# Suffix sums of stick-breaking attention: products of a rounded high and a low part in place of plain fp32 products

## The chip, the cores and the metric

The kernel runs on one NeuronCore of a Trainium2 chip. The metric is the device time of one execution in microseconds (us). TensorE (PE in the profile, with its weight loads as PEld), VectorE (DVE), ScalarE (ACT), GpSimd (POOL) and SyncE (SP, which issues the weight loads from memory) work from queues of their own, in order, and wait for each other on semaphores.

## The reference, cut to what matters

Two transformer blocks on 256 tokens of width 1024, in fp32. The change is in one mixer of the second block, stick-breaking attention with 8 heads of 128:

```
z = einsum('bqhd,bkhd->bhqk', q[:, lo:hi], k[:, :hi]) * scale
strict = arange(hi)[None, :] < (lo + arange(BLOCK_Q))[:, None]
log_fail = where(strict, -softplus(z), 0.0)
excl = cumsum(log_fail, axis=3, reverse=True) - log_fail
a = where(strict, exp(log_sigmoid(z) + excl), 0.0)
out = einsum('bhqk,bkhd->bqhd', a, v[:, :hi])
```

The reversed cumulative sum over the keys is the suffix sum. The kernel takes it as a product with a fixed 128x128 matrix: keys lie on the partitions, queries along the free axis, and each entry of the product is minus the sum of the softplus values of the keys from its own on.

## The kernel before, in words

The work is a list of phases; each phase has a method for each engine, and each engine goes through the phases in order. Weight products are made from two fp32r parts of each operand (`mm3`, lines 429 to 431: high by high, high by low, low by high). ScalarE rounds a chunk of weights of 128x2048 (L371), VectorE subtracts to get the low part (L379), and TensorE uses the chunk; four chunks are in the ring.

The phase of the change is `Stick`. Per head g it has causal tiles of 384 columns: 256 queries against the first 128 keys, 128 queries against the last 128 keys. The stages of a head are:

- `score`, TensorE (L2071, L2072): the logits, into bankA.
- `mask`, VectorE (L2163): adds the mask, into `lg`.
- ScalarE (L2138 to L2140): Abs, Exp, Ln, into `pt`; then `soften`, VectorE (L2174): the softplus value, in `pt`.
- `suffix`, TensorE (L2081 to L2083): three fp32 products with the suffix matrix and the matrix of minus ones.
- `exponent`, VectorE (L2169): `lg` plus the sums; then ScalarE (L2151): Exp, the attention weights.
- `value`, TensorE (L2097, L2098); after a pair of heads `take_hi` (ScalarE, L2103) and `take_lo` (VectorE, L2109) split the output.

The queues are written out by hand, a loop over g on each engine. In step g TensorE does score g+1, a filler, suffix g, value g-1. VectorE does exponent g-1, soften g, mask g+1, then the low part of a weight chunk (in steps 0, 1, 3, 5, 8) or `take_lo`; in step 7 soften stands ahead of the exponent. ScalarE does Abs, Exp, Ln of head g, in step 0 the rounding of a chunk, then the weights of head g-1 (which wait for exponent g-1), then the copies (L1604) and chunk roundings of the fillers, then `take_hi`; in step 7 a filler's copy stands ahead of the weights.

The fillers are the value and key projections of the next memory attention (`Fill`): one quarter, 12 products of 512 columns, in TensorE's queue before the loop and in each of the steps 0 to 6. Step 7 has none, and no score, since score 7 is in step 6. Step 8 has the transposes of the keys (L1598), ahead of value 7. After the phase comes `sb_out`, the output projection, with products of 512 columns again.

Of the kernel before, what the change touches and what calls it, by code (L numbers as in the profile page):

```python
# [17 lines left out]
F32 = mybir.dt.float32  # L18
F32R = mybir.dt.float32r
I32 = mybir.dt.int32  # L20
ALU = mybir.AluOpType
ACT = mybir.ActivationFunctionType
AX = mybir.AxisListType

P = 128
S = 256
# [12 lines left out]
H2, HD2 = 8, 128  # L39
# [73 lines left out]
C_ID, C_CAUSAL, C_STRICT, C_SUFFIX, C_ONES, C_FREQ, C_BUCK = 0, 128, 384, 768, 896, 1024, 1056  # L113
# [119 lines left out]
def build(nc, dram, out):  # L233
    ctx = ExitStack()
    with ctx:
        def sb(name, shape, dt=F32):
            return ctx.enter_context(nc.sbuf_tensor(name, shape, dt))

        def sem(name):
            return ctx.enter_context(nc.semaphore(name))  # L240
# [15 lines left out]
        qt = sb("qt", [P, KC, S])  # L256
        kt = sb("kt", [P, KC, S])
        v = sb("v", [P, NT, D])
        pet = sb("pet", [P, 6, S])
        rel = sb("rel", [P, 16, S])  # L260
        mem = rel[:, 8:16].rearrange("p (t a) s -> p t (a s)", t=NT)
# [3 lines left out]
        pt = sb("pt", [P, 2, TW])  # L265
        score = sb("score", [P, NT, S])
        const = sb("const", [P, C_BUCK])
# [10 lines left out]
        wi = sb("wi", [P, NT, NPARTS])  # L278
        trig = sb("trig", [P, 2, NT, HALF])
        pos = sb("pos", [P, 4])  # L280

        ps = ctx.enter_context(nc.psum_tensor("ps", [P, 8, TW], F32))
        bankA = [ps[:, 0], ps[:, 1]]
        bankT = [ps[:, 2], ps[:, 3]]
# [37 lines left out]
        def own(eng, counter, ins):  # L322

            eng.wait_ge(counter.sem, counter.inc(ins))
# [87 lines left out]
        def next_hi(act, n):  # L412

            if n + RING < len(PLAN):
                split_hi(act, n + RING)

        def next_lo(dve, n):
            if n + RING < len(PLAN):
                split_lo(dve, n + RING)
# [47 lines left out]
        def norm_scalar(act, name, half):  # L467
            for pair in (2 * half, 2 * half + 1):
                pair_scalar(act, name, pair)
# [10 lines left out]
        def rms_scalar(act, name):  # L480

            c = 2 * NORM[name]
            source_ready(act, name, 1)
            for t in range(NT):
                last = nc.scalar.activation(lg[:, :, :].rearrange("p a n -> p (a n)"), h[:, t], ACT.Square,
                                            scale=D ** -0.5, accum_out=ms[:, c + t:c + t + 1])
                if t == 0:
                    own(act, act_own, last)
            last.then_inc(ms_ready, 1)
# [86 lines left out]
        class Ffn:  # L576
# [274 lines left out]
            def scalar(self, act):  # L851
                if not self.gated:
                    next_hi(act, self.n0)
                rms_scalar(act, self.name)
                if self.gated:
                    next_hi(act, self.n0)
                if self.gated and self.name != "ffn1":
                    nc.scalar.preload_act_table(ACT.Silu)
                if self.gated:
                    act.wait_ge(rs_ready, RMS_AT[self.name])  # L860
                else:
                    act.wait_ge(ms_ready, RMS_AT[self.name])
                self.take_up_scalar(act, 0)
                for c in range(1, 4):
                    next_hi(act, self.n0 + c)
                if self.name == "ffn1":
                    tables.bias_scalar(act)
                for i in range(1, self.steps):
                    self.step_scalar(act, i, self.n0 + 4 * i)
                    if self.name == "ffn1" and i == 3:  # L870
                        tables.scalar(act)
                    if self.name == "ffn2" and i == 3:
                        mem_root.squares(act)
                if not self.following:
                    return
                chunks = [self.n0 + 4 * self.steps + c for c in range(4)]
                for half, n in enumerate(chunks[:2]):
                    next_hi(act, n)
                    norm_scalar(act, self.following, half)
                if self.following == "mla":  # L880
                    next_hi(act, chunks.pop(2))
                if self.following:
                    rms_scalar(act, self.following)
                for n in chunks[2:]:
                    next_hi(act, n)
# [751 lines left out]
        def fill_steps(fillers, g):  # L1637

            return [(f, step) for f in fillers for step, at in enumerate(f.groups) if at == g]
# [412 lines left out]
        class Stick:  # L2052
            def __init__(self, name, need, fillers):

                self.need, self.fillers = need, fillers
                self.scores = sem(name + "_scores")
                self.masked = sem(name + "_masked")
                self.logs = sem(name + "_logs")
                self.soft = sem(name + "_soft")
                self.sums = sem(name + "_sums")  # L2060
                self.expo = sem(name + "_expo")
                self.weights = sem(name + "_weights")
                self.summed = sem(name + "_summed")
                self.hi = sem(name + "_hi")
                self.lo = sem(name + "_lo")
# [7 lines left out]
                                 start=True, stop=True).then_inc(self.scores, 1)  # L2073

            def suffix(self, pe, g):
                pe.wait_ge(self.soft, g + 1)
                if g >= 2:
                    pe.wait_ge(self.expo, g - 1)
                suffix, ones = const[:, C_SUFFIX:C_SUFFIX + P], const[:, C_ONES:C_ONES + P]
                bank = bankT[g % 2]  # L2080
                nc.tensor.matmul(bank[:, 0:S], suffix, pt[:, g % 2, 0:S], start=True, stop=False)  # L2081
                nc.tensor.matmul(bank[:, P:S], ones, pt[:, g % 2, S:S + P], start=False, stop=True)
                nc.tensor.matmul(bank[:, S:S + P], suffix, pt[:, g % 2, S:S + P],  # L2083
                                 start=True, stop=True).then_inc(self.sums, 1)

            def pair_bank(self, pair):
                return bankD[0][pair % 2]
# [41 lines left out]
                        self.value(pe, g - 1)  # L2129

            def scalar(self, act):
                for g in range(H2 + 2):
                    if g < H2:
                        e = pt[:, g % 2, 0:S + P]
                        act.wait_ge(self.masked, g + 1)
                        if g >= 2:
                            act.wait_ge(self.sums, g - 1)
                        own(act, act_own, nc.scalar.activation(e, lg[:, g % 2, 0:S + P], ACT.Abs))  # L2138
                        own(act, act_own, nc.scalar.activation(e, e, ACT.Exp, scale=-1.0))
                        nc.scalar.activation(e, e, ACT.Ln, bias=one[:]).then_inc(self.logs, 1)  # L2140
                    if g == 0:
                        next_hi(act, self.last_chunk)
                    for filler, step in fill_steps(self.fillers, g):
                        if step == 8:
                            filler.scalar(act, step)
                    if 1 <= g <= H2:
                        b = (g - 1) % 2
                        act.wait_ge(self.expo, g)
                        if g >= 3:
                            act.wait_ge(self.summed, g - 2)  # L2150
                        nc.scalar.activation(nat[:, 1, b, 0:S + P], lg[:, b, 0:S + P], ACT.Exp)\  # L2151
                            .then_inc(self.weights, 1)
                    for filler, step in fill_steps(self.fillers, g):
                        if step != 8:
                            filler.scalar(act, step)
                    if g >= 3 and g % 2:
                        self.take_hi(act, g // 2 - 1)
# [20 lines left out]
            def vector(self, dve):  # L2178
                for g in range(H2 + 2):
                    if g == H2 - 1:  # L2180
                        self.soften(dve, g)
                    if 1 <= g <= H2:
                        self.exponent(dve, g - 1)
                    if g < H2 - 1:
                        self.soften(dve, g)
                    if g + 1 < H2:
                        self.mask(dve, g + 1)
                    if g == 0:
                        next_lo(dve, self.last_chunk)
                    if g >= 4 and g % 2 == 0:  # L2190
                        self.take_lo(dve, g // 2 - 2)
                    if g == H2 + 1:
                        self.take_lo(dve, H2 // 2 - 1)
                    for filler, step in fill_steps(self.fillers, g):
                        filler.vector(dve, step)
# [915 lines left out]
```

## Time and profile before

| | |
|---|---|
| median of 3 runs | 1266.13 us (1265.6 to 1266.35) |
| span of the profiled execution | 1264.6 us |
| time of that execution outside its span | not given; the three runs lie 1.0 to 1.75 us above the span |
| PE busy | 99% of the span |
| DVE, ACT busy | 60%, 52% |
| stick phase, from the first score to `sb_out` | 979.6 to 1020.3 us of the span |

Times of rows are counted from the start of the span. An instruction's row gives its start, its length, and in brackets how long its engine had been idle before it and on whom it waited. Matmuls overlap: what one costs TensorE is the distance from its start to the next one's start, and its length is more than that. On ScalarE and VectorE too the next instruction can start a little before the end of the last.

### The profile page before, as it was taken

To read this page: it belongs to the slowest core of one execution; us is meant where nothing else is said; L and a number is where in the kernel's file an instruction comes from. 1 tells how busy PE (TensorE), PEld (TensorE's weight loads), DVE (VectorE), ACT (ScalarE), POOL (GpSimd) and SP (SyncE) were. 2 spreads that over 40 slices of the span, in tenths; PEclk is the share of its full clock that TensorE was granted. 3 is DMA by queue.
4 is the path that set the end of the run, shared out by engine and by line. 5 is a ranking of instruction groups with operands and counts; after the bars stand their busy time and mean duration, and the time that the engine had idled before them with its cause. 6 is when DMAs were issued, how large, how long until landed. Compare 5 with 4: busy or idle time off the path is not lost.

```text
span 1264.6 us, 17026 instructions
## 1 busy us (share of the span) xinstructions
PE 1254.7 (99%) x6856; PEld 1087.0 (86%) x6856; DVE 763.8 (60%) x1084; ACT 652.4 (52%) x844; POOL 16.9 (1%) x21
## 2 busy tenths in 40 slices
PE   9999999999999999999999999999999999999998
PEld 7888888888888888889988899999888888999896
DVE  6555448888675654547875675454553656754554
ACT  6454437465455454446864563443555755643443
POOL 0000000001000000000000000000000000000001
PEclk9999999999999999999999999999999999999999
DMA  8855545654533655545643265553565332665530
GB/s 297 290 179 195 187 149 206 224 183 135 183 131 128 233 191 184 190 134 175 215 152 117 84 248 190 195 188 131 182 233 185 115 107 93 230 217 176 195 134 34
DMA packets 39486, 221.74 MB, mean 175 GB/s; under 512 B 4501, under 2 KB 5669, under 8 KB 23920
## 3 DMA queue, kind: packets, MB, share of 16 engines
q1 hardware_dynamic: 36800, 213.94, 49.4%
q0 software_dynamic: 1024, 4.22, 1.1%
q10 hardware_dynamic: 1584, 2.48, 0.7%
q8 instruction: 55, 0.90, 0.3%
q14 instruction: 23, 0.19, 0.0%
HBM read 219.56 MB, written 1.07 MB: 174 GB/s over the span
## 4 chain that ended last, share of the span: by engine, by line
PE 96%; ACT 2%; DVE 1%; issue 1%; ACTq 0%; DVEq 0%
PE ps L429 23%; PE ps L431 23%; PE ps L430 23%; PE ps L672 5%; PE ps L671 5%; PE ps L670 5%; PE ps L1728 2%; PE ps L1750 2%; PE ps L463 1%; PE ps L1737 1%; PE ps L708 1%; PE ps L1117 1%; ACT whi L371 1%; PE ps L2461 1%; PE ps L2463 1%; PE ps L2462 1%
## 5 line engine op out<-in xcount | busy, mean ns | idle before, releaser
L379 DVE TENSOR_TENSOR wlo<-w_raw,whi 128x2048 fp32r<-128x2048 f32 (+3 forms) x238 | 458.6, 1933 | 373.9 <-ACT whi L371 373.7
L371 ACT ACTIVATE whi<-w_raw 128x2048 fp32r<-128x2048 f32 (+4 forms) x242 | 390.8, 1622 | 404.1 <-PE ps L431 302.9
L429 PE MATMUL ps<-whi,xt_h 128*128 128x512 f32 (+3 forms) x740 | 291.0, 393 | 0.6 <-DVE wlo L403 0.2
L431 PE MATMUL ps<-whi,xt_l 128*128 128x512 f32 (+3 forms) x740 | 285.2, 385 | 0.0
L430 PE MATMUL ps<-wlo,xt_h 128*128 128x512 f32 (+3 forms) x740 | 284.6, 385 | 0.0
L429 PE MATMUL ps<-whi,ot_h 128*128 128x512 f32 x570 | 225.2, 395 | 0.0
L431 PE MATMUL ps<-whi,ot_l 128*128 128x512 f32 x570 | 222.3, 390 | 0.0
L430 PE MATMUL ps<-wlo,ot_h 128*128 128x512 f32 x570 | 222.1, 390 | 0.0
L429 PEld LDWEIGHTS ps<-whi,xt_h 128*128 128x128 f32 x740 | 139.0, 188 | 29.9 <-issue 3.9
L431 PEld LDWEIGHTS ps<-whi,xt_l 128*128 128x128 f32 x740 | 138.9, 188 | 27.7
L430 PEld LDWEIGHTS ps<-wlo,xt_h 128*128 128x128 f32 x740 | 139.1, 188 | 25.9
L670 PE MATMUL ps<-xt_h,whi 128*128 128x256 f32 x512 | 145.0, 283 | 0.0
L672 PE MATMUL ps<-xt_l,whi 128*128 128x256 f32 x512 | 144.9, 283 | 0.0
L671 PE MATMUL ps<-xt_h,wlo 128*128 128x256 f32 x512 | 144.9, 283 | 0.0
L431 PEld LDWEIGHTS ps<-whi,ot_l 128*128 128x128 f32 x570 | 107.0, 188 | 22.7
L430 PEld LDWEIGHTS ps<-wlo,ot_h 128*128 128x128 f32 x570 | 107.2, 188 | 20.9
L429 PEld LDWEIGHTS ps<-whi,ot_h 128*128 128x128 f32 x570 | 107.1, 188 | 20.8
L671 PEld LDWEIGHTS ps<-xt_h,wlo 128*128 128x128 f32 x512 | 98.2, 192 | 0.6
L670 PEld LDWEIGHTS ps<-xt_h,whi 128*128 128x128 f32 x512 | 98.2, 192 | 0.5
L672 PEld LDWEIGHTS ps<-xt_l,whi 128*128 128x128 f32 x512 | 98.2, 192 | 0.0
L476 ACT ACTIVATE xt_h<-ps,gain 128x256 fp32r<-128x256 f32 x88 | 34.5, 479 | 56.4 <-PE ps L463 56.4
L529 DVE SCALAR_TENSOR_TENSOR xt_l<-ps,gain,xt_h 128x256 fp32r<-128x256 f32 x88 | 36.5, 477 | 29.3 <-ACT xt_h L476 29.3
(264 smaller groups left out, 1055.2 us busy)
## 6 DMA issues: line engine op xcount, KB each, us to landing
w_raw<-ffn_mid SPq DMA_DIRECT2D x80, 768.0 KB, 4.3
w_raw<-mlp_mid SPq DMA_DIRECT2D x56, 1024.0 KB, 5.0
w_raw<-w_qkv SPq DMA_DIRECT2D x12, 1024.0 KB, 5.4
w_raw<-w_sb_qkv SPq DMA_DIRECT2D x12, 1024.0 KB, 5.0
w_raw<-w_xkv SPq DMA_DIRECT2D x8, 1024.0 KB, 5.0
w_raw<-ffn_first SPq DMA_DIRECT2D x8, 512.0 KB, 4.2
w_raw<-w_gate_b SPq DMA_DIRECT2D x4, 1024.0 KB, 5.0
w_raw<-w_gate_a SPq DMA_DIRECT2D x4, 1024.0 KB, 5.1
```

The costliest lines, as they stand in the source:

```text
L371: nc.scalar.activation(whi[:, s, 0:tiles * width], w_raw[:, s, 0:tiles * width], ACT.Copy).then_inc(w_hi, 1)
L379: nc.vector.tensor_tensor(wlo[:, s, 0:tiles * width], w_raw[:, s, 0:tiles * width], whi[:, s, 0:tiles * width].bitcast(F32), ALU.subtract) ...
L429: nc.tensor.matmul(acc, hi, whi[:, s, c], start=start, stop=False)
L430: nc.tensor.matmul(acc, hi, wlo[:, s, c], start=False, stop=False)
L431: return nc.tensor.matmul(acc, lo, whi[:, s, c], start=False, stop=stop)
L476: last = nc.scalar.activation(to[:, k], bank[:, j * S:(j + 1) * S], ACT.Copy, scale=gain[:, 8 * NORM[name] + k:8 * NORM[name] + k + 1])
L529: last = nc.vector.scalar_tensor_tensor(out=lo[:, k], in0=bank[:, j * S:(j + 1) * S], scalar=g, in1=hi[:, k].bitcast(F32), op0=ALU.mult, o ...
L670: nc.tensor.matmul(acc, whi[:, s, c], xt_h[:, k], start=k == 0, stop=False)
L671: nc.tensor.matmul(acc, wlo[:, s, c], xt_h[:, k], start=False, stop=False)
L672: last = nc.tensor.matmul(acc, whi[:, s, c], xt_l[:, k], start=False, stop=k == KC - 1)
L1728: last = nc.tensor.matmul(self.bank(g)[:, head["at"]:head["at"] + head["width"]], q, k, start=i == 0, stop=i == len(head["qk"]) - 1)
L1750: last = nc.tensor.matmul(head["out"], left, right, start=i == 0, stop=i == len(head["v"]) - 1)
```

## The change

The suffix sums are taken from two fp32r parts of the softened logits. ScalarE rounds `pt` to a high part (`soft_high`), VectorE subtracts it from `pt` for a low part (`soft_low`), each 128x384, and TensorE does four fp32r products: suffix matrix by the high part (384 columns), minus ones by the last 128 columns of the high part, then, after a wait for the low part, the same two with the low part. Before it were three fp32 products of 256, 128 and 128 columns. The fixed matrices are copied once into an fp32r tile (`sums_r`, 256 columns) at the head of ScalarE's part of the phase. The parts lie where `pet` lies, which the phase does not use.

```diff
+        with nc.sbuf_tensor("soft_hl", [P, 2, 2, S + P], F32R) as soft_hl:
+            pass
...
+        sums_r = sb("sums_r", [P, 2 * P], F32R)
...
             def suffix(self, pe, g):
-                pe.wait_ge(self.soft, g + 1)
+                pe.wait_ge(self.soft_hi, g + 1)
                 if g >= 2:
                     pe.wait_ge(self.expo, g - 1)
-                suffix, ones = const[:, C_SUFFIX:C_SUFFIX + P], const[:, C_ONES:C_ONES + P]
-                bank = bankT[g % 2]
-                nc.tensor.matmul(bank[:, 0:S], suffix, pt[:, g % 2, 0:S], start=True, stop=False)
-                nc.tensor.matmul(bank[:, P:S], ones, pt[:, g % 2, S:S + P], start=False, stop=True)
-                nc.tensor.matmul(bank[:, S:S + P], suffix, pt[:, g % 2, S:S + P],
-                                 start=True, stop=True).then_inc(self.sums, 1)
+                suffix, ones = sums_r[:, 0:P], sums_r[:, P:2 * P]
+                bank, hi, lo = bankT[g % 2], soft_hl[:, 0, g % 2], soft_hl[:, 1, g % 2]
+                nc.tensor.matmul(bank[:, 0:S + P], suffix, hi, start=True, stop=False)
+                nc.tensor.matmul(bank[:, P:S], ones, hi[:, S:S + P], start=False, stop=False)
+                pe.wait_ge(self.soft_lo, g + 1)
+                nc.tensor.matmul(bank[:, P:S], ones, lo[:, S:S + P], start=False, stop=False)
+                nc.tensor.matmul(bank[:, 0:S + P], suffix, lo, start=False, stop=True).then_inc(self.sums, 1)
+
+            def soft_high(self, act, g):
+                act.wait_ge(self.soft, g + 1)
+                nc.scalar.activation(soft_hl[:, 0, g % 2], pt[:, g % 2, 0:S + P], ACT.Copy).then_inc(self.soft_hi, 1)
+
+            def soft_low(self, dve, g):
+                dve.wait_ge(self.soft_hi, g + 1)
+                nc.vector.tensor_tensor(soft_hl[:, 1, g % 2], pt[:, g % 2, 0:S + P],
+                                        soft_hl[:, 0, g % 2].bitcast(F32), ALU.subtract).then_inc(self.soft_lo, 1)
...
             def scalar(self, act):
+                nc.scalar.activation(sums_r[:], const[:, C_SUFFIX:C_SUFFIX + 2 * P], ACT.Copy)
                 for g in range(H2 + 2):
...
                         nc.scalar.activation(nat[:, 1, b, 0:S + P], lg[:, b, 0:S + P], ACT.Exp)\
                             .then_inc(self.weights, 1)
+                    if g < H2:
+                        self.soft_high(act, g)
                     for filler, step in fill_steps(self.fillers, g):
...
                     if g + 1 < H2:
                         self.mask(dve, g + 1)
+                    if g < H2:
+                        self.soft_low(dve, g)
```

In step g `soft_high` thus stands behind the weights of head g-1 and ahead of the fillers' work; `soft_low` stands behind mask g+1 and ahead of the low part of a weight chunk.

## Rows read from the trace of the kernel before

**Rows 1.** The page: span, busy time of TensorE, and its granted clock in tenths.
```profile
span 1264.6 us, 17026 instructions
...
PE 1254.7 (99%) x6856; PEld 1087.0 (86%) x6856; DVE 763.8 (60%) x1084; ACT 652.4 (52%) x844; POOL 16.9 (1%) x21
...
PEclk9999999999999999999999999999999999999999
```

**Rows 2.** Timeline of TensorE, suffix 0 and score 2: start us, length us, engine, line.
```profile
986.82 0.59 PE L2081 MATMUL ps<-pt,const 128*128 128x256 f32 x2
...
987.47 0.39 PE L2083 MATMUL ps<-pt,const 128*128 128x128 f32 x2
987.69 0.60 PE L2071 MATMUL ps<-qt,kt 128*128 128x256 f32 x2
```

**Rows 3.** Timeline of TensorE, fp32r products of 384 columns at 583 us.
```profile
582.92 0.33 PE L429 MATMUL ps<-whi,xt_h 128*128 128x384 f32 x1
...
583.44 0.33 PE L429 MATMUL ps<-whi,xt_h 128*128 128x384 f32 x1
```

**Rows 4.** Timeline of TensorE, eight 64-column records, weights of 128 columns each.
```profile
342.26 1.00 PE L1750 MATMUL ps<-v,pt 128*128 128x64 f32 x8
343.07 0.48 PE L429 MATMUL ps<-whi,xt_h 128*128 128x512 f32 x1
```

**Rows 5.** Timeline of ScalarE in the stick phase (steps 0, 1 and 7).
```profile
983.33 1.90 ACT L371 ACTIVATE whi<-w_raw 128x2048 fp32r<-128x2048 f32 x1
...
988.48 0.53 ACT L2151 ACTIVATE nat<-lg 128x384 f32<-128x384 f32 x1 [1.63 <-DVE lg L2169]
988.91 1.90 ACT L371 ACTIVATE whi<-w_raw 128x2048 fp32r<-128x2048 f32 x1
...
1012.70 0.52 ACT L2151 ACTIVATE nat<-lg 128x384 f32<-128x384 f32 x1 [0.73 <-DVE lg L2169]
```

**Rows 6.** Timeline of VectorE in the stick phase (steps 0 to 2 and 7).
```profile
985.26 2.29 DVE L379 TENSOR_TENSOR wlo<-w_raw,whi 128x2048 fp32r<-128x2048 f32 x1 [0.78 <-ACT whi L371]
987.89 0.56 DVE L2169 TENSOR_TENSOR lg<-lg,ps 128x384 f32<-128x384 f32 x1 [0.34 <-PE ps L2083]
...
993.05 0.55 DVE L2169 TENSOR_TENSOR lg<-lg,ps 128x384 f32<-128x384 f32 x1
...
1015.69 0.56 DVE L2174 SCALAR_TENSOR_TENSOR pt<-lg,pt 128x384 f32<-128x384 f32 x1 [1.20 <-ACT pt L2140]
1016.82 0.56 DVE L2169 TENSOR_TENSOR lg<-lg,ps 128x384 f32<-128x384 f32 x1 [0.58 <-PE ps L2083]
```

**Rows 7.** Timeline of TensorE: starts of suffix 2, 6 and 7, and the phase's end.
```profile
996.02 0.59 PE L2081 MATMUL ps<-pt,const 128*128 128x256 f32 x2
...
1015.75 0.59 PE L2081 MATMUL ps<-pt,const 128*128 128x256 f32 x2
...
1017.28 0.60 PE L2081 MATMUL ps<-pt,const 128*128 128x256 f32 x2
...
1018.81 1.04 PE L1598 MATMUL ps<-const,nat 128*128 128x128 f32 x8
...
1020.26 0.47 PE L429 MATMUL ps<-whi,ot_h 128*128 128x512 f32 x1
```

**Rows 8.** Timeline: TensorE starts again after waiting for VectorE.
```profile
979.53 1.66 DVE L529 SCALAR_TENSOR_TENSOR xt_l<-ps,gain,xt_h 128x256 fp32r<-128x256 f32 x4 [2.60 <-ACT xt_h L476]
...
981.24 0.50 PE L429 MATMUL ps<-whi,xt_h 128*128 128x512 f32 x1
981.58 0.40 PE L430 MATMUL ps<-wlo,xt_h 128*128 128x512 f32 x1
981.82 0.39 PE L431 MATMUL ps<-whi,xt_l 128*128 128x512 f32 x1
```

**Rows 9.** Timeline of weight loads at the program's start, 256-column fp32 products.
```profile
1.19 3.06 PEld L3087 LDWEIGHTS ps<-lg 128*128 128x128 f32 x8 [1.19 <-DVE one L3070]
...
5.41 2.15 PEld L3087 LDWEIGHTS ps<-lg 128*128 128x128 f32 x6
```

More of the change, by code:

```diff
@@ L2059, in __init__ @@
                 self.soft = sem(name + "_soft")
+                self.soft_hi = sem(name + "_soft_hi")
+                self.soft_lo = sem(name + "_soft_lo")
                 self.sums = sem(name + "_sums")
```

## The prediction

> **What bounds the kernel now.** I read the page first: TensorE is busy for 99% of the span, at the full granted clock throughout [rows 1]. Then the waits of TensorE: between 979 and 1040 us there is only the restart at 981.24 [rows 8]. So in the stick phase TensorE's own queue sets the end, and a microsecond off it is a microsecond off the kernel, as long as ScalarE and VectorE deliver in time. Last, the timelines of the three engines, read side by side: which stage of a head is ready how long before TensorE comes to it. The reader should look there for slack, since the change lengthens the way from one suffix to the next.
>
> **What TensorE saves.** The three fp32 products of a head last from 986.82 to 987.69, 0.87 us [rows 2]; each is two records. Of the new four, the two of 384 columns cost 0.17 each: four starts lie between 582.92 and 583.44, three distances, 0.173 [rows 3]. An fp32r product of 128 columns stands nowhere in the trace. Eight 64-column records take 0.81 us, 0.10 each [rows 4]; at the 0.84 ns per column of the 256-column fp32 record (0.215 [rows 2]) their columns would be 0.054 each, so the weight load of 128 columns sets that distance and I take 0.11 for 128 columns too. Bounds: 0.066, if the columns alone counted (0.173 less 256 columns at 2.4 GHz), and 0.22, the whole fp32 product of 128 columns from 987.47 to 987.69 [rows 2]. So a head costs 2 x 0.173 + 2 x 0.11 = 0.57 in place of 0.87: 0.31 less (0.39 by the lower bound, 0.08 by the upper), and 8 heads 2.45 us less (3.1 and 0.7).
>
> The Trainium skill ("TensorE: Matmul & The Clock Gate", Back-to-back issue gap) gives some 81 ns for a sustained stream of 128-column products and 131 ns for 512. By the first the saving would be an estimated 2.9 us. The same passage's 131 ns for 512 columns is not what this kernel shows, where 512-column products start 0.23 to 0.24 us apart (981.58 and 981.82 [rows 8]).
>
> **What is added elsewhere.** ScalarE: a copy of 384 columns per head. The nearest row is the Exp of the same shape, 0.53 us, after which the next instruction starts 0.43 on (988.48 to 988.91) [rows 5]; I take 0.52 and 0.43. VectorE: a subtraction of 384 columns, like the exponent's addition, 0.56, the next some 0.09 before its end [rows 6]. Per head ScalarE gets 0.43 and VectorE 0.47 more work. Once, at the phase's head, the copy of the fixed matrices: 0.40 by the slope between 384 and 2048 columns (0.53 and 1.90) [rows 5]. No DMA is added, and no table load, because Copy already runs between Exp and Ln here in the fillers' copies. The engines are only about two thirds busy in this phase, but order counts: soft_high stands behind the weights of the head before, which wait for that head's exponent, which waits for that head's suffix. So after suffix g-1 there come, one after another, exponent (0.56), weights (0.53), high part (0.52), low part (0.56). TensorE covers this with value, score and a filler quarter of 2.7 us in steps 1 to 6. In step 7 it has only value 5 (0.65).
>
> A handing on between engines costs 0.03 (the chunk rounding of 983.33 ends at 985.23, its low part starts at 985.26 [rows 5, 6]). TensorE restarts 0.16 after its producer: VectorE ends at 981.19, the first two products start at 981.24 and 981.58, which is a stream of 0.23 distances begun at 981.35 [rows 8].
>
> **Following the queues step by step.** Times are starts. I write each queue down from 981.35 on with the lengths above, once for the kernel before and once for the change; for before this gives suffix 2 at 996.18 and `sb_out` at 1020.57, 0.16 and 0.31 behind the records [rows 7]. TensorE's due times below are on that scale, and the balance is the difference within it.
>
> - Step 0: the copy of the fixed matrices moves Abs 0, and so the chunk rounding from 983.33 to 983.55 [rows 5]. High 0 comes behind it at 985.36, low 0 at 985.91, and behind that the chunk's low part at 986.4 instead of 985.26 [rows 6]. It blocks exponent 0, 988.6 instead of 987.89. TensorE has soft parts in time (due 986.94) and loses nothing.
> - Step 1: the weights 0 at 989.2, high 1 989.64, the chunk rounding 990.07 instead of 988.91 [rows 5], its low part 992.0 to 994.3, exponent 1 at 994.2 instead of 993.05 [rows 6]. Suffix 1 has its parts (low 1 ends 990.8, due 991.2).
> - Step 2: behind exponent 1, soften 2 ends at 995.2, high 2 runs 995.26 to 995.78, low 2 to 996.38. TensorE, two suffixes at 0.31 ahead, is due at 995.56 against 996.18. It waits 0.38 for the high part, then 0.32 for the low part.
> - Step 4: the chunk of step 3 is late in the same way (rounding 999.7, low part to 1003.9), high 4 ends 1005.37, just in time, low 4 1005.97; a wait of 0.31. Steps 3, 5 and 6 have no wait.
> - Step 7: ScalarE begins weights 5 at 1013.03 (before 1012.70 [rows 5]); then high 6, a filler's copy, Abs, Exp and Ln of head 7, which ends at 1016.25. Soften 7 thus starts at 1016.28 in place of 1015.69 [rows 6], and exponent 6 stands behind it, 1016.75. Then weights 6 at 1017.34, high 7 1017.78 to 1018.30, TensorE from 1018.46; it was due at 1016.35, after value 5. A wait of 2.11, and 0.31 for low 7.
>
> Behind it, exponent 7 and weights 7 (to 1020.65) are covered by value 6 and the eight transposes, which take 0.87 (eight records from 1018.81 [rows 7]). take_lo 2, which `sb_out` awaits, ends at 1020.7, before TensorE gets there. The last chunk rounded in the phase is wanted three chunks later, 16 us, so its delay of 1 us is hidden.
>
> **Sum.** Saved 2.45; waits 0.38 + 0.32 + 0.31 + 2.11 + 0.31 = 3.43. Balance +0.98, less a few hundredths of rounding: +0.95. `sb_out` starts at 1021.2 instead of 1020.26 [rows 7]. From there all queues move by the same amount, so the span becomes 1264.6 + 0.95 = 1265.5; the runs' median stands 1.53 above the span, which gives 1267.1. This hardly hangs on the unknown price. With 0.066 the saving is 3.1 and the waits 4.1, +0.9, because TensorE only comes earlier to the same waits; with 0.22 it is 0.7 against 1.8, +1.1. The measurement tells nothing within 0.2% (2.5 us), so the forecast is: no change that can be told.
>
> **Rivals.**
>
> *Only the unavoidable wait remains (a small gain).* If ScalarE and VectorE are not late (shorter instructions than I take, other overlaps), the waits in steps 2 and 4 vanish and step 7 costs the bare chain: the last product of suffix 6 gives its sums at 1015.86, exponent at 1015.9, weights 6 1016.5, high 7 1016.9 to 1017.4, TensorE 1017.6 instead of 1016.35, then 0.31: 1.56. Balance -0.9, span 1263.7, time 1265.2; with 0.066 for the short products -1.6. For it: exponent 6 was held by its suffix alone before (idle 0.58 [rows 6]). Against it: each chunk's low part blocks an exponent already now (no idle ahead of 993.05 [rows 6]). For more than 0.2% faster the chain of step 7 would have to be hidden too, for which there is nothing in TensorE's queue.
>
> *The clock falls (slower).* A TensorE that stands for over 2 us at 1016.4 could be granted the 1.2 GHz level for a while. The row that prices it is the program's start: eight and then six fp32 records of 256 columns at 0.38 and 0.36 each, against 0.215 [rows 2, 9], over 6.4 us, so some 2.7 us lost. Added to +0.95 that makes +3.7, time 1269.8. It decides if the stretch of low clock exceeds about 3 us. For: it follows directly on the longest wait. Against: the waits of 0.2 to 0.5 us in this trace leave the granted clock at full, but none is as long as this one, so they exclude little. The Trainium skill (same page, The HAM clock gate) says that lack of activity brings the array back to 1.2 GHz; by that rule this rival is possible here, and the trace of before neither shows nor excludes it.
>
> *The products get no cheaper.* Were four fp32r products as dear as three fp32 ones, TensorE would save nothing, and would come later to each wait: only step 7's remains, 1.28 + 0.15, +1.4, time 1267.6. That is still no change that can be told. Against it stands the distance of 0.173 for 384 columns [rows 3], so this can concern the short products alone.
>
> **How the numbers follow.** The forecast (waits eat the saving) 0.66; small gain 0.12; products no cheaper 0.04; clock 0.10; the chain hidden after all or other savings, beyond 0.2% faster, 0.05; other delays beyond 0.2% slower (a chunk late in `sb_out`), 0.03. Faster than 0.2%: 0.05. Slower: 0.13. Same: 0.82. The forecast's own range is 1266.2 to 1268.3 (each of some ten lengths in the chain uncertain by 0.05 to 0.1). The range for 8 in 10 leaves out the clock and the hidden chain and takes in the small gain: 1264.8 to 1268.9.
>
> **What would show it.** TensorE's records of the suffix: four per head, 0.57 in all where it does not wait. TensorE idle for about 2 us ahead of suffix 7, released by ScalarE's high part, and for 0.3 to 0.7 at suffixes 2 and 4. Exponent 1 a microsecond later than 993.05. A granted clock that stays full behind 1018. The forecast is wrong if TensorE has no idle in step 7, if the clock falls there, or if a product behind 1021 waits for a weight chunk.

## The result, and the profile after

| | before | after |
|---|---|---|
| median of 21 runs each | 1266.27 us | 1268.75 us (1267.38 to 1269.67) |
| span of the profiled execution | 1264.6 us | 1265.6 us |
| ratio of the times | | 1.0018, 95% interval 1.0012 to 1.0024 |

The kernel is slower: by 2.5 us between the medians, by 0.18% in the ratio, which is taken over all executions. The profiled span shows only 1.0 us of it. The difference is in the list of executions: 8 of the 21 have spans of 1265.4 to 1265.7 us, at a mean granted clock of 0.999, and 13 have 1266.5 to 1267.6, at 0.997 or 0.998. The profiled execution is one of the 8 short ones. The mean clock alone does not tell the groups apart elsewhere, since 0.998 stands beside short spans too (1264.2 in an experiment below); it is the spans that form two groups. Before has one group, 1263.6 to 1265.1 in 61 executions beside the experiments below, around 1264.4.

The page of the changed kernel, in the lines of [rows 1]:

```profile
span 1265.6 us, 17011 instructions
...
PE 1253.4 (99%) x6840; PEld 1084.5 (86%) x6840; DVE 767.8 (61%) x1092; ACT 656.0 (52%) x853; POOL 16.9 (1%) x21
...
PEclk9999999999999999999999999999999999999999
```

TensorE is busy 1.3 us less and the span is 1.0 longer. The waits of TensorE over the whole span, by line, in us in total, times, longest:

```profile
PE ps L2086 <- ACT soft_hl L2095: 2.0, 2, 1.8
PE ps L3109 <- DVE one L3092: 1.2, 1, 1.2
PE ps L1740 <- DVE lg L1826: 0.8, 3, 0.4
...
PE ps L2089 <- DVE soft_hl L2100: 0.2, 1, 0.2
```

The first and the last line are new: L2086 is the first product with a high part, L2089 the first with a low part. The timeline of TensorE at suffix 0, where nothing is late (before: [rows 2]):

```profile
986.72 0.34 PE L2086 MATMUL ps<-soft_hl,sums_r 128*128 128x384 f32 x1
986.90 0.22 PE L2087 MATMUL ps<-soft_hl,sums_r 128*128 128x128 f32 x1
986.96 0.27 PE L2089 MATMUL ps<-soft_hl,sums_r 128*128 128x128 f32 x1
987.07 0.39 PE L2090 MATMUL ps<-soft_hl,sums_r 128*128 128x384 f32 x1
987.30 0.59 PE L2076 MATMUL ps<-qt,kt 128*128 128x256 f32 x2
```

From 986.72 to 987.30 it is 0.58 us instead of 0.87: the saving is there, 0.29 a head, 2.3 us in eight heads. The same timeline from value 5 to `sb_out` (before: [rows 7]):

```profile
1016.00 0.38 PE L2115 MATMUL ps<-nat,v 128*128 128x128 f32 x2
1018.19 0.45 PE L2086 MATMUL ps<-soft_hl,sums_r 128*128 128x384 f32 x1 [1.81 <-ACT soft_hl L2095]
1018.48 0.22 PE L2087 MATMUL ps<-soft_hl,sums_r 128*128 128x128 f32 x1
1018.79 0.33 PE L2089 MATMUL ps<-soft_hl,sums_r 128*128 128x128 f32 x1
...
1019.18 0.59 PE L2114 MATMUL ps<-nat,v 128*128 128x256 f32 x2
...
1021.28 0.48 PE L432 MATMUL ps<-whi,ot_h 128*128 128x512 f32 x1
```

and why suffix 7 is late, in ScalarE's timeline:

```profile
1015.50 0.62 ACT L2158 ACTIVATE pt<-pt,one 128x384 f32<-128x384 f32 x1
1016.02 0.67 ACT L1607 ACTIVATE nat<-ps,rs 128x512 f32<-128x512 f32 x1
1017.21 0.52 ACT L2169 ACTIVATE nat<-lg 128x384 f32<-128x384 f32 x1 [0.51 <-DVE lg L2189]
1017.63 0.51 ACT L2095 ACTIVATE soft_hl<-pt 128x384 fp32r<-128x384 f32 x1
```

and in VectorE's:

```profile
1016.15 0.56 DVE L2194 SCALAR_TENSOR_TENSOR pt<-lg,pt 128x384 f32<-128x384 f32 x1 [0.97 <-ACT pt L2158]
1016.62 0.55 DVE L2189 TENSOR_TENSOR lg<-lg,ps 128x384 f32<-128x384 f32 x1
1018.17 0.56 DVE L2100 TENSOR_TENSOR soft_hl<-pt,soft_hl 128x384 fp32r<-128x384 f32 x1 [1.00 <-ACT soft_hl L2095]
```

Read them as a chain: Ln 7, soften 7 (1016.15), exponent 6 behind it with no idle (1016.62), weights 6 (1017.21), high 7 (1017.63), and then TensorE (1018.19) and low 7 (1018.17). The high part itself could have been made from 1016.71 on, when soften 7 ended; it stood in the queue behind weights 6.

### The profile page after: what moved, and what is told of

Read it like the earlier page. It is cut to its first block, busy times and chain, and to the rows that moved or that the text cites. A ratio compares the mean times of both kernels' runs of the same rounds, so it can differ in the third digit from the quotient of the medians.

```text
span 1265.6 us, 17011 instructions
## 1 busy us (share of the span) xinstructions
PE 1253.4 (99%) x6840; PEld 1084.5 (86%) x6840; DVE 767.8 (61%) x1092; ACT 656.0 (52%) x853; POOL 16.9 (1%) x21
## 4 chain that ended last, share of the span: by engine, by line
PE 94%; ACT 3%; DVE 2%; issue 1%; ACTq 0%; DVEq 0%
PE ps L432 23%; PE ps L434 22%; PE ps L433 22%; PE ps L675 5%; PE ps L674 5%; PE ps L673 5%; PE ps L1731 2%; PE ps L1753 2%; PE ps L466 1%; ACT whi L374 1%; PE ps L1740 1%; PE ps L711 1%; PE ps L1120 1%; PE ps L2483 1%; PE ps L2485 1%
```

## The experiments

The theory after the result, A: the waits are those of the prediction, in every execution, and the long executions are those in which TensorE's clock falls after the wait ahead of suffix 7. The rivals to it are B, the extra time is spread over the program, and others named at each run. The kernel before was measured beside them in 61 executions, with medians of 1266.22 (the first four experiments) and 1266.20 us (the last four). One execution of each experiment was profiled; that the others of a run are of the same kind is inferred from their spans.

### The changed kernel once more

No edit.

> The changed kernel once more, unchanged. It moves the median by 2.5 us but the profiled span by only 1.0 us. Theory A (queues and clock): every execution has the same waits, of which the one ahead of suffix 7 (1.8 us of TensorE idle) is followed in some executions by a stretch at the lower granted clock. Then the spans lie in two groups, near 1265.5 (clock 0.999) and 1266.5 to 1267.6 (0.998 or 0.997), and if the profiled execution is of the second group its trace shows granted clock under 1.00 just behind 1018 us and nowhere else that before does not have. Theory B: the extra time is spread over the kernel (transfers, jitter of a changed program); then spans form no two groups, or the trace of a long one shows full clock behind 1018 us.

Measured: median 1268.83 us, ratio 1.0019 (1.0010 to 1.0028); 4 executions with spans of 1265.5 to 1265.9, 7 with 1266.6 to 1267.8. This time the profiled execution is the longest, 1267.8. Its windows of half a microsecond: stretch, its length, busy time of TensorE, granted clock, share of the DMA engines, GB/s:

```profile
1019.00:1019.50 0.50, 0.41 (x3) 1.00 0.00 0
1019.50:1020.00 0.50, 0.50 (x4) 0.98 0.00 0
1020.00:1020.50 0.50, 0.50 (x3) 0.50 0.00 0
...
1022.50:1023.00 0.50, 0.50 (x3) 0.50 0.00 0
1023.00:1023.50 0.50, 0.50 (x5) 0.60 0.00 0
1023.50:1024.00 0.50, 0.50 (x5) 1.00 0.00 0
```

and its timeline of TensorE:

```profile
1018.75 0.44 PE L2086 MATMUL ps<-soft_hl,sums_r 128*128 128x384 f32 x1 [1.80 <-ACT soft_hl L2095]
...
1019.73 0.80 PE L2114 MATMUL ps<-nat,v 128*128 128x256 f32 x2
...
1020.76 1.91 PE L1601 MATMUL ps<-const,nat 128*128 128x128 f32 x8
1022.46 1.06 PE L2114 MATMUL ps<-nat,v 128*128 128x256 f32 x2
...
1023.50 0.47 PE L432 MATMUL ps<-whi,ot_h 128*128 128x512 f32 x1
```

For some 3.4 us, 1020.0 to 1023.4, the granted clock is half, the 1.2 GHz level. The eight transposes take 1.70 (1020.76 to 1022.46) instead of 0.88. From value 6 to `sb_out` it is 3.77 us, where the short execution needs 2.10 (1019.18 to 1021.28): 1.7 us lost. In all other stretches of 20 us the granted clock is 1.00. The wait itself is the same, 1.80.

The span is 2.2 us longer than that of the short profile, so 0.5 more has to be found. It lies at the program's start: suffix 0 already starts 0.57 later (987.29 against 986.72), and this trace has a wait ahead of a first weight product, at 8.1 us, that the short one lacks:

```profile
PE ps L646 <- ACT whi L390: 0.7, 1, 0.7
```

Four of the other profiles have that wait too, 0.2 to 0.9 long, and over the ten profiles suffix 0 starts anywhere from 986.07 to 987.29. This spread arises long before the changed phase, in whose waits it has no part. So theory B falls for the larger part: 1.7 of the 2.2 us are in one place, behind the wait ahead of suffix 7. The other six long executions of this run were not profiled; they are taken to be of the same kind.

### The high part of head 7 earlier

```diff
+                    if g == H2 - 1:
+                        self.soft_high(act, g)
                     if 1 <= g <= H2:
                         b = (g - 1) % 2
                         act.wait_ge(self.expo, g)
...
-                    if g < H2:
+                    if g < H2 - 1:
                         self.soft_high(act, g)
```

> In step 7 the high part of head 7 stands ahead of the weights of head 6 in ScalarE's queue; everything else as in the changed kernel. Theory A: the high part no longer waits for exponent 6 and weights 6, the wait ahead of suffix 7 shrinks from 2.0 to about 1.1 us, the first product of sb_out starts 0.9 us earlier, the span is 1264.7, and with the shorter idle the long group of spans becomes rare, so the median drops by 1 to 3 us against the changed kernel, to about 1266. Rival (the wait of step 7 is hidden by something behind it, for example the last weight chunk): no change, 1268.7. Rival to the clock: a drop of 0.9 us only, with both groups of spans as frequent as before.

Measured: median 1266.60 us, ratio to before 1.0003 (0.9994 to 1.0012), spans 1264.2 to 1264.9 in all 11, no long group. The profiled span is 1264.6. TensorE's timeline:

```profile
1015.94 0.38 PE L2115 MATMUL ps<-nat,v 128*128 128x128 f32 x2
1017.25 0.45 PE L2086 MATMUL ps<-soft_hl,sums_r 128*128 128x384 f32 x1 [0.93 <-ACT soft_hl L2095]
```

The idle is 0.93 instead of 1.81, `sb_out` starts 0.9 earlier, and the median falls by 2.2 us: 0.9 for the wait and the rest because no execution is long any more. One moved instruction takes back nearly all that the change had cost.

### The products alone

```diff
-                bank, hi, lo = bankT[g % 2], soft_hl[:, 0, g % 2], soft_hl[:, 1, g % 2]
+                bank, hi, lo = bankT[g % 2], soft_hl[:, 0, g % 2], soft_hl[:, 0, g % 2]
...
-                    out=pt[:, g % 2, 0:S + P], in0=lg[:, g % 2, 0:S + P], scalar=0.0,
+                    out=soft_hl[:, 0, g % 2], in0=lg[:, g % 2, 0:S + P], scalar=0.0,
...
-                        self.soft_high(act, g)
...
-                        self.soft_low(dve, g)
```

The waits on the high and low part are gone too; the suffix waits for `soft` as before. This kernel leaves the low part out, so it is a probe of the time and not a version to use.

> The four fp32r products without the splitting: VectorE writes the softened logits straight as a rounded high part, and both pairs of products read it (the low part is left out, the high part counts twice). ScalarE and VectorE have no more work per head than before the change. Theory A: TensorE's saving of about 0.3 us a head comes through, 2.3 us, less some 0.3 us of a wait for weights 6 in the last steps: about 2.0 us faster than before, 1264.2, in one group of spans with no lowered clock. Rival (fp32r products save nothing, or the saving is taken back further on): within 0.5 us of before.

Measured: 1264.17 us, ratio 0.9984 (0.9975 to 0.9993), 2.05 us faster than before. Its timeline at suffix 7:

```profile
1015.52 0.39 PE L2089 MATMUL ps<-soft_hl,sums_r 128*128 128x384 f32 x1
1015.88 0.70 PE L2113 MATMUL ps<-nat,v 128*128 128x256 f32 x2
```

Ten of the 11 spans lie at 1261.9 to 1262.5, one at 1263.3. The products' saving is real and reaches the end. The distance of 0.36 ahead of value 6, against 0.23 elsewhere, is a small wait; by its place it is for weights 6 (they end at 1015.82), which TensorE had covered with its dearer products before.

### The splitting alone

```diff
-                suffix, ones = sums_r[:, 0:P], sums_r[:, P:2 * P]
...
+                nc.tensor.matmul(bank[:, 0:S], suffix, pt[:, g % 2, 0:S], start=True, stop=False)
                 pe.wait_ge(self.soft_lo, g + 1)
+                nc.tensor.matmul(bank[:, P:S], ones, pt[:, g % 2, S:S + P], start=False, stop=True)
+                nc.tensor.matmul(bank[:, S:S + P], suffix, pt[:, g % 2, S:S + P],
+                                 start=True, stop=True).then_inc(self.sums, 1)
```

> The splitting without its use: ScalarE's high part and VectorE's low part are made and waited for as in the changed kernel, but the products are the three fp32 ones of before. Theory A: nothing is saved, TensorE comes later to each wait, only step 7's wait remains (1.4 us in all), and the span is 1.4 us above before's, 1266.0; the idle ahead of suffix 7 is shorter (about 1.2 us), so the long group of spans should be rarer than in the changed kernel, time 1267.5 to 1268. Rival (the splits cost through their own time on ScalarE and VectorE at every head, 8 times about 0.5 us): 4 us above before.

Measured: 1267.93 us, ratio 1.0014 (1.0005 to 1.0022), spans 1265.4 to 1266.3, median 1266.0, 1.6 above before's 1264.4. TensorE's waits:

```profile
PE ps L2086 <- ACT soft_hl L2095: 1.0, 1, 1.0
```

The only wait for a part is that of step 7, at 1.0 of idle. So the splits cost nothing by the time that they take on ScalarE and VectorE, which would have shown at every head. None of the 11 executions is long, since their spans lie within 0.9 us. The two halves do not add up to the whole: -2.1 and +1.6 in the spans would be -0.5, where the short executions of the changed kernel stand at +1.2. The 1.7 between them is saving that TensorE only spends in longer waits.

### The wait filled with work that nobody reads

```diff
+                    if g == H2 - 1:
+                        pe.wait_ge(self.masked, g)
+                        for _ in range(4):
+                            nc.tensor.matmul(bankA[0][:, 0:S], ident, const[:, 0:S], start=True, stop=True)
                     if g < H2:
                         self.suffix(pe, g)
```

> The changed kernel, and in step 7, between value 5 and suffix 7, TensorE does four more fp32 products of 256 columns that nobody reads (0.43 us each, 1.7 us in all), so that it works through the 1.8 us in which it idles in the changed kernel. The way from suffix 6 over ScalarE and VectorE to suffix 7 stays as it is. Theory A (the idle itself makes the clock fall in some executions): the first product of sb_out starts at the same time as in the changed kernel's short executions, all spans lie in one group near 1265.6, the trace has full granted clock behind 1018 us, and the median falls by 1.2 us to about 1267.6, although TensorE has more work. Rival (the two groups have another cause): two groups as before, median 1268.8. Rival (TensorE's work counts): 1.7 us above the changed kernel.

Measured: 1267.42 us, ratio 1.0010 (1.0000 to 1.0019); spans 1264.9 to 1266.1, median 1265.5, no long group. The timeline:

```profile
1016.25 1.89 PE L2146 MATMUL ps<-const 128*128 128x256 f32 x8
1018.21 0.44 PE L2086 MATMUL ps<-soft_hl,sums_r 128*128 128x384 f32 x1
...
1021.29 0.48 PE L432 MATMUL ps<-whi,ot_h 128*128 128x512 f32 x1
```

Suffix 7 and `sb_out` start as in the short execution of the changed kernel (1018.19, 1021.28). TensorE does 1.7 us more work, and the median is 1.4 us less; the granted clock of the profiled execution is 1.00 from 1016 to 1027. This is the cleanest of the tests: the path over ScalarE and VectorE is untouched, only TensorE's idleness is gone, and with it the long group of spans.

### The wait made longer

```diff
+                    if g == H2 - 1:
+                        act.wait_ge(self.soft, g + 1)
+                        for _ in range(2):
+                            own(act, act_own, nc.scalar.activation(soft_hl[:, 0, g % 2], pt[:, g % 2, 0:S + P],
+                                                                   ACT.Copy))
                     if g < H2:
                         self.soft_high(act, g)
```

> The changed kernel with the high part of head 7 written three times by ScalarE (each time the same), so the wait ahead of suffix 7 is 1.1 us longer, about 2.9 us of idle. Theory A: span 1266.6 where the clock stays full, and the lower granted clock behind suffix 7 comes in every or nearly every execution instead of in about six of ten, at 1 to 2 us each: spans 1268 to 1269, median near 1270.3. Rival (the clock has nothing to do with the wait's length): the same share of long executions as in the changed kernel, median 1269.9 at most with the short group at 1268.6.

Measured: 1270.05 us in 6 executions, ratio 1.0030 (1.0019 to 1.0042), spans 1267.7 to 1269.1, all at a mean clock of 0.997 or 0.998. TensorE's wait and the windows of the profiled one, columns as above:

```profile
PE ps L2086 <- ACT soft_hl L2095: 2.9, 1, 2.9
```

```profile
1019.50:1020.00 0.50, 0.41 (x4) 0.98 0.00 0
1020.00:1020.50 0.50, 0.50 (x3) 0.50 0.00 0
...
1023.00:1023.50 0.50, 0.50 (x4) 0.61 0.00 0
1023.50:1024.00 0.50, 0.50 (x6) 1.00 0.00 0
```

The profiled execution lost 1.7 us behind the wait again. The other spans are 1.1 us or more above the 1266.6 expected at full clock, so with 2.9 us of idle all six are taken as long; with 1.8 it was 20 of 32; with 0.9 and 1.0 none of 22.

### The chunk's low part later

On top of the early high part 7:

```diff
-                    for filler, step in fill_steps(self.fillers, g):
-                        filler.vector(dve, step)
+                    for filler, step in fill_steps(self.fillers, g - 1 if g == 2 else g):
+                        if g != 1:
+                            filler.vector(dve, step)
```

> The kernel of the early high part 7, and VectorE makes the low part of the filler's weight chunk of step 1 one step later, behind low part 2 of the softened logits. Theory A: exponent 1 is no longer blocked by the 2.3 us instruction, the parts of head 2 are ready ahead of TensorE, and the wait of 0.7 us at suffix 2 goes; 0.2 of it comes back at suffix 4. The span falls by 0.5 us to 1264.1, median 1266.1. Rival (waits in steps 2 and 4 cost nothing because step 7's wait swallows them): no change against the early high part, 1266.6.

Measured: 1266.01 us, ratio 0.9998 (0.9989 to 1.0007); median span 1264.1 against 1264.7. The timeline at suffix 1, 2 and 3:

```profile
990.37 0.34 PE L2086 MATMUL ps<-soft_hl,sums_r 128*128 128x384 f32 x1
...
995.01 0.34 PE L2086 MATMUL ps<-soft_hl,sums_r 128*128 128x384 f32 x1
...
999.65 0.34 PE L2086 MATMUL ps<-soft_hl,sums_r 128*128 128x384 f32 x1
```

Both distances are 4.64: the wait at suffix 2 is gone (in the changed kernel it made 4.98 of the first and, by its low part, 5.12 of the second). That is 0.83 less; the span falls by 0.6, since 0.25 comes back at suffix 4. There the two parts now cost 0.14 and 0.38 where it was 0 and 0.27, as expected: TensorE comes earlier to the same late parts.

### The filler's copies later as well

```diff
+                    if g == H2 - 1:
+                        self.fillers[1].copy(act, 0)
                     if g == H2 - 1:
                         self.soft_high(act, g)
...
                     for filler, step in fill_steps(self.fillers, g):
-                        if step != 8:
+                        if not (g == H2 - 2 and step == 4):
+                            filler.scalar(act, step)
```

The loop that did step 8 ahead of the weights is taken out, so that copy now stands behind them.

> As the run with the later low part, and ScalarE's two copies of the filler's keys stand one behind Ln 7 (where it waits for soften 7 anyway), the other behind the weights of head 6. Theory A: Abs, Exp and Ln of head 7 come 0.6 us earlier, exponent 6 is no longer held by soften 7, the wait ahead of suffix 7 shrinks by 0.3 us more, span 1263.8, median 1265.7: 0.5 us under the kernel before. Rival (the transposes of step 8 wait for the second copy): the gain is lost there, 1266.1.

Measured: 1265.93 us, ratio 0.9997 (0.9988 to 1.0005), median span 1263.8. From suffix 6 to suffix 7 it is 2.08 us (1014.58 to 1016.66) where the run before had 2.31 (1014.09 to 1016.40), so 0.23 of the expected 0.3 is there in the profile, and 0.3 in the median spans. The way was not the expected one: Ln 7 comes only 0.24 earlier and not 0.6 (0.26 behind the start of suffix 6 instead of 0.50), because Abs 7 now waits 0.22 for VectorE's mask, and exponent 6 still stands right behind soften 7 (1015.49 and 1015.96). The times differ by 0.1 only, which these runs cannot tell from nothing. This is the fastest version with the whole computation: 0.3 us under the kernel before, also within what can be told.

## Why the prediction was right, and where it was not

**The saving.** 0.31 a head was predicted, 0.29 measured. Where the trace of before had no row, for the 128-column product, the two fp32r records stand 0.06 (986.90 to 986.96) and 0.11 (986.96 to 987.07) from the next. The second 384-column product stands 0.23 from what follows, in place of 0.17. The sum of four, 0.58 where 0.57 had been taken, is right by luck: the errors of its parts cancel. The Trainium skill ("TensorE: Matmul & The Clock Gate", LDWEIGHTS) gives the nanoseconds of a weight load as columns over 1.2, so an estimated 107 for 128 columns. The trace agrees in the second distance (0.11), not in the first (0.06). The successor in the first has the same weights, but the trace has a load record for it too, so that the weights are the reason is not shown.

**The waits.** Taken as the distance between the starts of products, less the same distance at suffix 0, where nothing waits (0.40 from the last filler product to L2087, 0.06 and 0.11 behind that): at suffix 2 the high part costs 0.45 and the low part 0.38 (predicted 0.38 and 0.32), at suffix 4 the low part 0.27 (0.31), at suffix 7 2.07 and 0.30 (2.11 and 0.31); for suffix 7 the undisturbed distance from value 5 to L2087 is that of the products alone, 0.41. Together 3.47 against 3.43. These are TensorE's rows at suffix 2, and two of suffix 4, in the changed kernel:

```profile
995.13 0.39 PE L434 MATMUL ps<-whi,xt_l 128*128 128x512 f32 x1
995.70 0.44 PE L2086 MATMUL ps<-soft_hl,sums_r 128*128 128x384 f32 x1 [0.18 <-ACT soft_hl L2095]
995.98 0.22 PE L2087 MATMUL ps<-soft_hl,sums_r 128*128 128x128 f32 x1
996.36 0.33 PE L2089 MATMUL ps<-soft_hl,sums_r 128*128 128x128 f32 x1 [0.16 <-DVE soft_hl L2100]
996.53 0.39 PE L2090 MATMUL ps<-soft_hl,sums_r 128*128 128x384 f32 x1
...
1005.63 0.22 PE L2087 MATMUL ps<-soft_hl,sums_r 128*128 128x128 f32 x1
1005.90 0.33 PE L2089 MATMUL ps<-soft_hl,sums_r 128*128 128x128 f32 x1
```

**The walk through the queues.** High 7 was put at 1017.78 and stands at 1017.63, exponent 6 at 1016.75 and stands at 1016.62; both in an execution whose phase began 0.1 earlier. Exponent 1, delayed by the chunk's low part, was put at 994.2 and stands at 994.07. `sb_out` at 1021.28 is 1.02 later than in [rows 7], predicted 0.95. The single experiments took the sum apart: the products alone give -2.05 us, the splits alone +1.7, and moving single instructions gave about what was expected (0.9 of 0.9 at the start of `sb_out`, 0.6 of 0.5 and 0.3 of 0.3 in the median spans), the last of them in another way than expected and not told from nothing in the times.

**The step that failed is the clock's chance, not its mechanism.** The forecast, 1267.1, is the time of an execution in which the clock stays full; those are 12 of the 32 executions, at 1267.4 to 1267.9. The rival with the falling clock was given 1 in 10 and is what 20 of 32 do. Its price was put at 2.7 us and is 1.7 in the profiled one. The row that priced it, the program's start, was no row of a lowered clock: the trace of before gives a granted clock of 1.00 there, and the weight loads of its 256-column products lie 0.38 and 0.36 apart [rows 9], where at the half clock two such records take 0.86 (1022.46 to 1023.32), 0.43 each. Why the start is slow is not shown; that the figure served at all is luck. The median is that of the mixture, 1268.75, still within 0.2% of before by its point value (0.196%), but above the forecast's own range of 1266.2 to 1268.3. It lies 0.15 us below the top of the range for 8 in 10, which was drawn so as to leave the falling clock out: that it is inside is luck, and had the price been the 2.7 it would have been outside. The argument against the rival had been that waits up to 0.5 us leave the clock alone; as the prediction said, they excluded little, and it should have been weighed accordingly. The Trainium skill (same page, The HAM clock gate) says lack of activity brings the array back to 1.2 GHz; the traces agree, with half the granted clock from 1020.0 to 1023.4 after 1.8 us of idle.

**A smaller error.** The time was taken as 1.53 above the span. Over all runs before's time lies 1.8 above its span (1266.2 to 1264.4), and the short executions of the changed kernel 2.0 above theirs (1267.6 to 1265.6). The remaining 0.5 us of the forecast for the short ones (1267.1 against 1267.6) is this offset.

The rival "small gain" needed the engines to be on time; they were late by about as much as the walk had said. The rival "products no cheaper" is excluded by the 2.05 us of the products alone.

## What to carry to other kernels

Shortening products in a queue that covers a chain on other engines moves TensorE earlier to the same waits; walk the chain once per step of the loop, and look first at the step that has no filler. A new instruction belongs behind the last thing that it needs, not behind the last thing that stands in the loop's body: one instruction moved ahead of another gave back 2.2 us. And an idle stretch of TensorE costs more than its length once the clock falls behind it, so a median that moves more than the profiled span is a reason to look at the spans and clocks of all executions.

## What was unexpected of the hardware

- An idle of 1.8 us on a TensorE that had not idled for more than 0.4 us at a time in over 900 us can be followed by a stretch at the 1.2 GHz level, 3.4 us long in both executions that were profiled with it. By the spans it is there in 20 of 32 executions with 1.8 us of idle, in 6 of 6 with 2.9, and in none of 44 with 0.7 to 1.0. What decides it among executions with the same idle is not shown. The lowered stretch begins not at the idle but after TensorE has started again: in the two profiled cases at 1020.0, 1.2 and 0.8 us after suffix 7.
- Keeping TensorE busy with 1.7 us of products that nobody reads makes the kernel 1.4 us faster.
- Two fp32r products of 128 columns with the same weights start 0.06 us apart, though the trace has a weight-load record for each, where eight records of 64 columns had stood 0.10 apart [rows 4].
